# A streaming encoder layer: first loads reordered, first mixing operands loaded in the stage before, two matmul pieces moved within each tile

## The reference, cut to what matters

```
mod = silu(c) @ w_ada + b_ada                      # six rows of 1024 for each of 9 requests
h   = rmsnorm(x, ln1) * (1 + sc1) + sh1
qa, ka, va, qb, fb, ib, gb = split(h @ w_in)       # 1024 x 2816
oa  = windowed attention(qa, ka, va) with sinks and distance penalties
ob  = gated linear recurrence(qb, fb, ib), normed, times silu(gb)
x   = x + g1 * (concat(oa, ob) @ w_out)
h2  = rmsnorm(x, ln2) * (1 + sc2) + sh2
x   = x + g2 * moe(h2)                             # 16 experts, two chosen for each row
```

## Time and profile before

| | |
|---|---|
| three runs | 1403.38, 1406.37, 1411.02 us; median 1406.37 |
| the profiled execution | 1410.54 us, of which 1408.5 are the span from the first to the last instruction |
| mean granted clock of TensorE | 0.893 |
| busy share | PE 88%, DVE 52%, ACT 39%, POOL 26% |
| DMA | 249.87 MB, mean 177 GB/s |

### The profile page before, as it was taken

How to read it: one execution, slowest core, us unless ns; L and a number is a source line. 1 busy time by engine, 2 the same in 40 slices (tenths; PEclk the granted TensorE clock), 3 DMA queues, 4 the chain that set the end, 5 groups by cost and what they waited for, 6 DMA issues and landing times. The chain is left out here.

```text
span 1408.5 us, 21648 instructions
## 1 busy us (share of the span) xinstructions
PE 1238.9 (88%) x7081; PEld 1022.5 (73%) x7082; DVE 737.7 (52%) x1066; ACT 550.8 (39%) x921; POOL 365.7 (26%) x419
## 2 busy tenths in 40 slices
PE   3789999999595999999999816999999999879964
PEld 1568889988464888888888715788887887668853
DVE  2553510342553666756666466552555585655851
ACT  3363421323322434444444203441444465444640
POOL 1000200122502433433433012233323332433222
PEclk8799999999666998989988956999999999989987
DMA  9626773512256323303321166387759889887864
GB/s 352 215 90 206 253 277 108 162 51 70 70 144 191 102 72 101 102 31 102 102 72 46 34 220 243 135 270 197 249 179 312 275 283 371 268 288 254 268 242 89
DMA packets 119430, 249.87 MB, mean 177 GB/s; under 512 B 17713, under 2 KB 47153, under 8 KB 116290
## 3 DMA queue, kind: packets, MB, share of 16 engines
q1 hardware_dynamic: 107266, 204.92, 41.9%
q0 software_dynamic: 12096, 44.05, 12.0%
HBM read 205.02 MB, written 43.93 MB: 177 GB/s over the span
## 5 line engine op out<-in xcount | busy, mean ns | idle before, releaser
L2106 PE MATMUL psum<-e_w_h,e_x_h 128*128 128x512 f32 x432 | 173.8, 402 | 30.5 <-DVE w_gu L2219 23.7
L2108 PE MATMUL psum<-e_w_h,e_x_l 128*128 128x512 f32 x432 | 171.0, 396 | 0.0
L2107 PE MATMUL psum<-w_gu,e_x_h 128*128 x432 | 170.6, 395 | 0.0
L2053 POOL DMA_INDIRECT out<-e_work,e_to x26 | 87.9, 3380 | 302.1 <-DVE e_work L2207 302.1
L2219 DVE TENSOR_TENSOR w_gu<-w_gu,e_w_h 128x1024 f32 x128 | 146.7, 1217 | 21.1 <-ACT e_w_h L2160 21.1
L2160 ACT ACTIVATE e_w_h<-w_gu 128x1024 fp32r x128 | 123.0, 1048 | 54.5 <-issue 33.3
L2106 PEld LDWEIGHTS psum<-e_w_h,e_x_h 128*128 128x128 f32 x432 | 82.8, 192 | 48.7 <-DVE w_gu L2219 24.1
L498 PE MATMUL psum<-p_w_h,p_h_h 128*128 128x512 f32 (+1 forms) x288 | 107.4, 373 | 1.6 <-DVE p_h_l L653 1.6
L500 PE MATMUL psum<-p_w_h,p_h_l 128*128 128x512 f32 (+1 forms) x288 | 106.8, 371 | 0.0
L499 PE MATMUL psum<-p_w_l,p_h_h 128*128 128x512 f32 (+1 forms) x288 | 106.7, 371 | 0.0
L2108 PEld LDWEIGHTS psum<-e_w_h,e_x_l 128*128 128x128 f32 x432 | 82.5, 191 | 17.8
(11 more groups left out here) (367 smaller groups left out, 2661.5 us busy)
## 6 DMA issues: line engine op xcount, KB each, us to landing
w_gu<-in_w_e_gate SPq DMA_DIRECT2D x16, 2048.0 KB, 15.4
w_gu<-in_w_e_up SPq DMA_DIRECT2D x16, 2048.0 KB, 19.3
w_dn<-in_w_e_down SPq DMA_DIRECT2D x16, 2048.0 KB, 15.5
shared<-in_w_ada SPq DMA_DIRECT2D x24, 1024.0 KB, 6.6
p_w_raw<-in_w_in SPq DMA_DIRECT2D x5, 2048.0 KB, 9.3
m_feat<-feat_d SPq DMA_DIRECT2D x8, 1024.0 KB, 6.6
m_tok<-tok_d SPq DMA_DIRECT2D x8, 896.0 KB, 8.9
tok_d<-p_tok SPq DMA_DIRECT2D x27, 256.0 KB, 2.0
```

The source lines that it names most:

```text
L2053: pool.indirect_dma_start(out=d["y"], out_offset=bass.IndirectOffsetOnAxis(ap=to_now[1 - par][:, 0:1], axis=0), in_=y_s[:, 1 - par, :], in ...
L2106: pe.matmul(psum[:, j, :], x_h[:, k, :], wh, start=(k == 0), stop=False)
L2107: pe.matmul(psum[:, j, :], x_h[:, k, :], wl, start=False, stop=False)
L2108: last = pe.matmul(psum[:, j, :], x_l[:, k, :], wh, start=False, stop=(k == KC - 1))
```

## The change

Three edits. First, SP's order at the head of `projection`: the bias and ln1 come right behind the first three chunks; then chunks 3 to 7, w_in group 0 and x tile 1; w_in group 1 comes behind the wait for the first modulation row and the load of ln2. Second, the first tile's `feat` and `tok` get buffers that live through `sampling` and `mixing`, and SP issues their loads in `sampling`, ahead of the wait for the state; two buffers of `sampling` (`pn_t`, `o_sq`) now share the memory of others (`cache_t`, `kd_tok`). Third, in TensorE's program `fill` 6 stands behind the turning of k_d, and `fill` 7 behind the state matmuls.

```diff
@@ projection, SP
             for i in range(STAGES):
                 load_stage(i)
-            load_x(1)
-            load_w(0)
-            for i in range(STAGES, KC):
-                load_stage(i)
             for j in range(4):
                 sp.dma_start(bias4[32 * j:32 * j + 32, :, :], ...)
             with nc.allow_non_contiguous_dma("a column of ln1 for each chunk"):
                 sp.dma_start(ln1_t[:, :], ...)
-            load_w(1)
+            for i in range(STAGES, KC):
+                load_stage(i)
+            load_w(0)
+            load_x(1)
             sp.dma_start(o_norm_w[:, :], ...)
...
             sp.wait_ge(s["row_done"], 1)
             for j in range(2):
                 sp.dma_start(ln2_row[32 * j:32 * j + 32, :], ...)
+            load_w(1)
@@ new helpers
+def load_feat(sp, d, t, feat, loaded):
+    sp.dma_start(feat[:, :, :].rearrange("p a (c r) -> p (a c) r", r=P),
+                 d["feat"][:, :, :, t * P:(t + 1) * P].rearrange("p a c r -> p (a c) r")).then_inc(loaded, 16)
+def load_tok(sp, d, t, tok, loaded):
+    sp.dma_start(tok[:, :], d["tok"][t * P:(t + 1) * P, :]).then_inc(loaded, 16)
@@ sampling
-        pn_t = sb("pn_t", [L, 8, P])
+        pn_t = cache_t[0:L, :, :]
-        o_sq = sb("o_sq", [P, 8, HD])
+        o_sq = kd_tok[:, :].rearrange("p (h d) -> p h d", d=HD)
...
                 sp.dma_start(d["y"][ROWS:TABLE, half], zeros[:, :]).then_inc(s["operands_in"], 16)
+            load_feat(sp, d, 0, b["feat0"], b["feat0_loaded"])
+            load_tok(sp, d, 0, b["tok0"], b["tok0_loaded"])
             sp.wait_ge(s["state_ready"], 1)
@@ mixing, SP
-            load_tile(0)
             sp.dma_start(sink[:, :], sinks.partition_broadcast(P)).then_inc(s["sinks_loaded"], 16)
@@ mixing, TensorE
                 level(t, 5)
-                fill(t, 6)
                 values(t, 1)
                 level(t, 6)
                 pe.wait_ge(s["kexp_ready"], t + 1)
                 turn4(OB, k_d, s["kd_turned"])
-                fill(t, 7)
+                fill(t, 6)
                 if t + 1 < TP:
                     turn_qk(t + 1)
...
                 last.then_inc(s["state_mm"], 1)
+                fill(t, 7)
                 pe.wait_ge(s["oa_ready"], t + 1)
```

More of the change, by code:

```diff
@@ L169, in stream_layer @@
                 mix_p=sb(mid, "mix_p", [P, 2, KC, P]), w_oh=sb(mid, "w_oh", [P, KC, D], F32R),
-                w_r=sb(mid, "w_r", [P, KC, NE]))
+                w_r=sb(mid, "w_r", [P, KC, NE]), feat0=sb(mid, "feat0", [P, 4, QW]), tok0=sb(mid, "tok0", [P, TOK]),
+                feat0_loaded=sem("feat0_loaded"), tok0_loaded=sem("tok0_loaded"))
             sampling(nc, b, d, sinks, state_in, s_sample)
@@ L1113, in mixing @@
         table = b["shared"][:, :].rearrange("p (a i n) -> p a i n", a=3, i=2)
-        feat, tok = sb("feat", [P, 2, 4, QW]), sb("tok", [P, 2, TOK])
+        feat, tok = (b["feat0"], sb("feat1", [P, 4, QW])), (b["tok0"], sb("tok1", [P, TOK]))
         x_in, x2 = sb("x_in", [P, 2, D]), sb("x2", [P, 2, D])
@@ L1145, in mixing @@
         s = {n: sem(n) for n in names}
-        feat_loaded, tok_loaded, x_loaded, x2_stored = ([sem(f"{n}{i}") for i in range(2)]
-                                                        for n in ("feat_loaded", "tok_loaded", "x_loaded", "x2_stored"))
+        x_loaded, x2_stored = ([sem(f"{n}{i}") for i in range(2)] for n in ("x_loaded", "x2_stored"))
+        feat_loaded, tok_loaded = (b["feat0_loaded"], sem("feat1_loaded")), (b["tok0_loaded"], sem("tok1_loaded"))
         ctx.callback(retire, nc, sems)
@@ L1168, in fts @@
         def fts(t, i):
-            return feat[:, t % 2, i, :]
+            return feat[t % 2][:, i, :]
         def toks(t, a, n):
-            return tok[:, t % 2, a:a + n]
+            return tok[t % 2][:, a:a + n]
         def table_row(i, u):
@@ L1183, in load_tile @@
                     sp.wait_ge(s["kexp_ready"], t - 1)
-                sp.dma_start(feat[:, t % 2, :, :].rearrange("p a (c r) -> p (a c) r", r=P),
-                             d["feat"][:, :, :, rows(t)].rearrange("p a c r -> p (a c) r")).then_inc(feat_loaded[t % 2], 16)
+                load_feat(sp, d, t, feat[t % 2], feat_loaded[t % 2])
                 if t >= 2:
@@ L1188, in load_tile @@
                     sp.wait_ge(s["v_ready"], t - 1)
-                sp.dma_start(tok[:, t % 2, :], d["tok"][rows(t), :]).then_inc(tok_loaded[t % 2], 16)
+                load_tok(sp, d, t, tok[t % 2], tok_loaded[t % 2])
             def load_x(u):
```

## The result

The changed kernel takes 1410.99 us (median of 20 runs, 1400.24 to 1419.45), the kernel before 1405.18 us beside it (20 runs, 1398.91 to 1411.43). The ratio is 1.0034, with a 95% interval of 1.0017 to 1.005: some 4.8 us slower (the two medians lie 5.8 us apart). That is inside the 0.5% called no change, and inside the range; the interval leaves no doubt that the sign is a loss.

The account below looks back on a forecast made before the run. TensorE was taken as the bound, losing time standing still at stage heads or running at 1.2 instead of 2.4 GHz. Terms +6.5 - 6.3 + 0 = +0.2 us on 1406.4 gave 1406.6 us, range 1397 to 1417.

Parts of the forecast that it names:

- Edit 1, +6.5 predicted: Head of projection: late x tile 1 delays norm(1), weight splits and bias addition; first job 53.7 instead of 47.13, +6.5 us.
- Edit 2, -6.3 predicted: Head of mixing: POOL no longer waits for the features, so scores come at 442.66 instead of 448.97, -6.3 us.
- Edit 3, 0 predicted: Tile's end in mixing: moved pieces add no wait, 0 us; the clock could make it -14 to +9.
- 1.25 was the term: Tile's end: the residual waits for piece 7, later by the q and k turning and state matmuls, 1.25 us.
- The prediction's own sign of being wrong: In mixing's tiles: tiles of 38 us or less, or a clock fall ahead of piece 6, would refute it.
- a second fall: Between pieces 5 and 6, the clock falls again in each of eight tiles: +23 us, 1429; chance 0.10.
- Longer falls: In mixing's tiles, the three short clock falls become long: +9 us, 1415; chance 0.12.
- The sum: Whole kernel: +6.5 - 6.3 + 0 = +0.2 us, 1406.6 us, so no change; chance 0.50.
- shorter falls: In mixing's tiles, all five long clock falls become short: -14 us, 1392.5; chance 0.16.
- no new wait at the start: Head of projection: x tile 1 lands by some 30 us, bias addition keeps its time; -6.3 us, 1400; chance 0.12.

Follow-up runs that it names:

- the filled kernel with the same loads: The changed kernel with six unread 512-column matmuls added per tile (four in the last) and piece 4 interleaved with the logits: 1397.7 us, ratio 0.996.
- the first filled kernel: The kernel before with edit 2, reordered first loads and head programs, six unread matmuls more per tile, piece 4 among the logits: 1388.04 us, ratio 0.9901.
- The kernel with every tile at 41.0 us: The first filled kernel with three more unread matmuls in each tile but the first, among logits and first values: 1385.11 us, ratio 0.9847 to the kernel before.

## Why the prediction came out as it did

**Edit 1, +6.5 predicted: right in place and mechanism.** x tile 1 was put at 36.5 and landed at 36.36 (36.2 to 36.9 in the four kernels with this order); the bias addition at 45.1 and came at 44.77, the first job at 53.7 and came at 53.31. The 8.13 MB more in front of x tile 1 took 36.36 - 14.07 = 22.3 us; the sum had 22.45. Its slow stretch is the one that came with the bias and ln1: 0.99 MB in the 4 us from 13 to 17, 1.6 us more than at 409 GB/s. By bytes over 436 GB/s plus 2.0 us, as the Trainium skill has it ("DMA: Bandwidth & Descriptors", Anatomy of one DMA — SWDGE (gpsimd) path), x tile 1 would have been in at 30.4; it was not, and the rows had said so. The Trainium skill states that fit for one transfer issued by GpSimd; here more than a dozen stand in SP's queue. norm(2) runs at 56.97, as worked out, with no DMA in front of it. The timed runs give the edit 8 us, 2 more than these two traces. The kernel before's trace, from which the sum starts, is part of the reason. Four profiled executions have the old load order, and their first jobs are at 45.44 to 47.13, 46.4 on the mean, with this trace the latest; four have the new one, at 53.20 to 53.81, 53.5 on the mean. By those means edit 1 costs 7.0 us at the first job and 7.7 at the opening of sampling (367.8 and 375.5), so the term was about a microsecond short. The profiled execution of the changed kernel lost 2.1 us more between the first job and sampling, where TensorE waits 9.6 us for normalised rows instead of 7.1; the filled kernel with the same loads waits 7.4 there, so that is this execution's.

**Edit 2, -6.3 predicted: right.** 6.09 us by the trace of the changed kernel, 6.6 by the timed runs. The stage opening stayed where the state stores put it, and the sinks and the zero stores cost nothing that shows.

**Edit 3, 0 predicted, with the clock left open from -14 to +9: no wait, as worked out; a loss of 3 us as the mean of three readings, which the runs do not settle.** The residual moved as the sum had it: in the changed kernel its first half starts 3.56 us ahead of its reader, the turning of the attention output (621.67 and 625.23), before 4.84 (611.11 and 615.95). That is 1.28 later, and 1.25 was the term; it ends 2.33 us ahead of the reader, by the sum 2.35.

The step that failed is the sentence that the fall stays one in each tile, at its end. The prediction's own sign of being wrong, a clock that falls ahead of piece 6, is there at 508.9 and 556.7. The rival "a second fall" had the right kind of event at the wrong place and in the wrong number: it was put between pieces 5 and 6, in each of eight tiles, for 23 us. It came at the logits, and in one tile only of the profiled execution, besides a tile that has its one fall there. "Longer falls" does not describe it either: the other falls of the tiles are 3.4 to 13.7 us long, before 6.8 to 13.7.

Tiles over 45 us turn up in two of the four profiled executions with edit 3 and unfilled tiles (46.10 and 47.48 us, and 46.08 in the kernel with x tile 1 moved), and in none of the five without it. But all three unfilled executions that have a fall at the logits in their first tiles, one of them without edit 3, are those with both edit 2 and late first loads. Edit 3 with edit 2 alone, or with neither, brought on no such fall. So edit 3 is neither enough for it nor needed, by these single executions; whether it makes such falls longer (13.7 us in all three with it, 3.4 in the one without) stays open, and so does what puts them there: with edit 1 alone `mixing` opens at 443.32, as in the changed kernel at 443.65, and none comes.

**The sum.** +0.2 us predicted, +4.8 measured (0.17% to 0.5%). The excess is about 1.5 us of edit 1 and 3 us of edit 3, both inside their bounds, and neither resolved from zero by the timed runs. That the total came out inside the range is no merit of the zero for edit 3: edits 1 and 2 were right, and the range left room for either sign of the clock. Of the rivals, "shorter falls" and "no new wait at the start" were wrong: the falls are not shorter, and the wait at the start is there.

## What to carry to other kernels

Ahead of a reordering of loads, list for each engine what its program puts ahead of the instruction that the load is for: here the bias came sooner, and the bias addition later, because four splits stood ahead of it and waited for what had been moved back. With the engines' programs changed too, much the same loads brought the first job 6 us forward, where the new load order alone put it 6 back. And where a row of the clock is below full speed while TensorE has no idle time, try filling the thin matmuls before moving the dense ones about: 67 matmuls that compute nothing, with one piece spread among the logits, made the kernel some 12 us shorter.

## What the hardware showed unexpectedly

The clock fell to half with TensorE at work: at 508.9 it was in the logits (507.79 for 2.59 us, matmuls of 16 columns), behind a stretch of score and level matmuls. Its last waits ahead of that ended at 498.77 and 500.13, 0.65 us for VectorE and 0.25 for ACT; from there to the fall it has no idle time.

```profile
500.13 1.09 PE L1350 MATMUL psum<-ident,m_score 128*128 128x128 f32 x8 [0.25 <-ACT m_sink_e L1481]
```

The Trainium skill tells of falls from gaps in which TensorE waits for a DMA ("TensorE: Matmul & The Clock Gate", HAM oscillation); this fall has no such gap ahead of it. With 512-column matmuls among the logits and at the tile's end the falls within the tiles went, but for one. What it is in the added matmuls that does this is not shown: no run puts anything else in their places.

A fall that is taken away in one place can come up in another: with the tile's end filled, the two that were left in the first filled kernel began at the logits, where the kernel before had shown none. Whether the falls also spread the timed runs is not shown. The kernel with every tile at 41.0 us ranges over 5.6 us in six runs, but the kernel with edit 1 alone, which has its falls, ranges over 5.4 in six.
